# Sample states of a two-layer HGRN2 and SSD decoder step: the queries moved to four column tiles, the new states to two row tiles

## What is computed

```python
o_inter = jnp.einsum('bthk,bhkv->bthv', qb * jnp.exp(G), s)          # HGRN2, 4 heads, 128x128
s_new = jnp.exp(g_last)[..., None] * s + jnp.einsum('bshk,bshv->bhkv', k_dec, vb)
y_inter = jnp.einsum('btgn,bgrnp->btgrp', cb, hg) * jnp.exp(acum)[..., None]   # SSD, 8 heads, 128x64
h_new = jnp.exp(a_last)[..., None, None] * hg + jnp.einsum('bsgn,bsgrp->bgrnp', bb, xg * w[..., None])
```

## Time and profile before

| | |
|---|---|
| runs, us | 1828.41 median of 3 (1827.68 to 1837.21) |
| the profiled execution, us | 1836.97, its span 1835.2 |
| TensorE busy | 1779.1 us, 97% of the span |
| VectorE, ACT, GpSimd busy | 71%, 56%, 6% |
| mean granted TensorE clock | 0.963 |

### The profile page before, as it was taken

How to read it: one execution, slowest core, us unless ns; L and a number is a source line. 1 busy time by engine, 2 the same in 40 slices (tenths; PEclk the granted TensorE clock), 3 DMA queues, 4 the chain that set the end, 5 groups by cost and what they waited for, 6 DMA issues and landing times.

```text
span 1835.2 us, 23214 instructions
## 1 busy us (share of the span) xinstructions
PE 1779.1 (97%) x9594; PEld 1549.2 (84%) x9594; DVE 1296.9 (71%) x1099; ACT 1036.0 (56%) x934; POOL 112.1 (6%) x101
## 2 busy tenths in 40 slices
PE   8999999999999998998999999999999999899997
PEld 7988888999999978886888878888788888788886
DVE  6635555444347345547988888888988888788897
ACT  4443224333334342227777777777777777677776
POOL 2011120000000011210400000000000000000200
PEclk9998879999999978788999999999999999999999
DMA  9458144443453512137999999999999999899994
GB/s 291 160 180 241 35 111 147 141 158 107 137 172 116 161 40 54 41 90 257 380 395 395 394 363 387 365 375 393 375 362 363 370 397 378 297 383 365 383 385 186
DMA packets 272616, 474.20 MB, mean 258 GB/s; under 512 B 41578, under 2 KB 103266, under 8 KB 272504
## 3 DMA queue, kind: packets, MB, share of 16 engines
q1 hardware_dynamic: 266432, 452.50, 69.5%
q10 hardware_dynamic: 3368, 12.75, 2.1%
q0 software_dynamic: 2704, 7.39, 1.4%
HBM read 454.82 MB, written 29.84 MB: 264 GB/s over the span
## 4 chain that ended last, share of the span: by engine, by line
PE 93%; DVE 4%; ACT 1%; issue 1%; DMA 0%; DVEq 0%; ACTq 0%
PE ps L1676 17%; PE ps L1677 17%; PE ps L2297 11%; PE ps L1671 9%; PE ps L1672 9%; PE ps L2318 5%; PE ps L1770 4%; PE ps L2183 3%; PE ps L1880 3%; PE ps L1865 2%; PE ps L2201 1%; PE ps L2336 1%; PE ps L1918 1%; PE ps L2145 1%; PE ps L2035 1%
## 5 line engine op out<-in xcount | busy, mean ns | idle before, releaser
L1556 DVE TENSOR_TENSOR spL<-ring,spH 128x2048 fp32r<-128x2048 f32 x336 | 767.3, 2292 | 111.2 <-ACT spH L954 106.4
L954 ACT ACTIVATE spH<-ring 128x2048 fp32r<-128x2048 f32 x336 | 643.4, 1917 | 136.3 <-PE ps L2297 74.0
L1676 PE MATMUL ps<-spH,XH 128*128 128x512 f32 x896 | 356.5, 398 | 1.9 <-issue 1.9
L1677 PE MATMUL ps<-spH,XL 128*128 128x512 f32 x896 | 352.5, 393 | 2.3 <-issue 2.3
L1037 DVE TENSOR_TENSOR spL<-ring,spH 128x2048 fp32r<-128x2048 f32 (+1 forms) x74 | 158.8, 2146 | 182.3 <-ACT spH L660 182.1
L1671 PE MATMUL ps<-hnH,spH 128*128 128x320 f32 x928 | 277.3, 313 | 4.1 <-DVE hnL L1052 2.2
L1672 PE MATMUL ps<-hnL,spH 128*128 128x320 f32 x928 | 275.6, 311 | 0.0
L2297 PE MATMUL ps<-spL,XH 128*128 128x512 f32 x896 | 242.5, 393 | 0.2 <-DVE spL L1556 0.2
L660 ACT ACTIVATE spH<-ring 128x2048 fp32r<-128x2048 f32 (+1 forms) x74 | 133.4, 1803 | 187.9 <-PE ps L2183 73.6
L1677 PEld LDWEIGHTS ps<-spH,XL 128*128 128x128 f32 x896 | 169.0, 189 | 38.4 <-issue 2.7
L2297 PEld LDWEIGHTS ps<-spL,XH 128*128 128x128 f32 x896 | 168.6, 188 | 38.6 <-DVE spL L1556 0.9
(11 more groups left out here) (358 smaller groups left out, 1944.0 us busy)
## 6 DMA issues: line engine op xcount, KB each, us to landing
ring<-in_w_exp_in_dram SPq DMA_DIRECT2D x224, 1024.0 KB, 8.1
ring<-in_w_exp_out_dram SPq DMA_DIRECT2D x112, 1024.0 KB, 8.5
ring<-in_w_in_dram SPq DMA_DIRECT2D x28, 1024.0 KB, 5.3
ring<-in_w_ffn_in_dram SPq DMA_DIRECT2D x22, 1024.0 KB, 5.1
token_rows<-token_rows ACTq DMA_DIRECT2D x1, 11776.0 KB, 41.9
ring<-in_w_ffn_out_dram SPq DMA_DIRECT2D x16, 704.0 KB, 4.6
ring<-in_w_out_dram SPq DMA_DIRECT2D x8, 1024.0 KB, 5.1
out_dram<-ring SPq DMA_DIRECT2D x32, 256.0 KB, 2.6
```

Of the source, the lines that this page charges most:

```text
L954: A(esplit(j)[0], src, ACT.Copy).then_inc(S("hi_done"), 1)
L1556: V.tensor_tensor(lo, eslot(j)[0], hi.bitcast(F32), ALU.subtract).then_inc(S("split_done"), 1)
L1676: mm(out, x[0], w, start=start, stop=False)
L1677: return mm(out, x[1], w, start=False, stop=False)
```

## The change

Queries: `ask(k, half)` serves four sequences at once, in two calls per group k (0 HGRN2, 1 SSD). The stationary side is now a block of 32 query columns (four sequences), the moving side the slab's 128 columns; head h writes to partitions 32h to 32h+31 of bank 5, which is column tile h of the array. 16 matmuls a call; of each block of 32 rows only the 8 of the slab's own sequence are used. ACT copies bank 5 to `said` (`told`), TensorE turns it with four transposes (`turn_said`), VectorE adds it to oT (`add_told`) or multiplies it for SSD (`decay_told`). `ASK_AT` and `TOLD_AT` place these.

New states: one call per pair of sequences j and j+4. Rows 0 to 31 of keys and values hold sequences 0 to 3, rows 32 to 63 sequences 4 to 7, and the mask `turn` keeps j in the one and j+4 in the other; the two halves are two row tiles (32 rows x 128 columns) and write to banks 4 and 7. All calls use the same two banks, so `sample_state(j)` waits until both adds of j-1 are done, and `sample_ssd(j)` too. `sample_ssd(3)` stays behind `group_squares(1)`, and the adds that it waits for stand on VectorE behind the scaling of oT.

```diff
+    turn = ((i[:, None] // LSQ) % 4 == np.arange(4)[None, :]).astype(np.float32)
...
-SEQ_AT = {(0, 1): (0,), (0, 2): (1,), (0, 3): (2,), (1, 1): (3,), (1, 2): (4, 5), (1, 3): (6, 7)}
-SEQ_BANK = (4, 7, 7, 4, 7, 4, 7, 4)
-SSD_BANK = (7, 4, 7, 7, 4, 7, 4, 7)
+SEQ_AT = {(0, 3): 0, (1, 1): 1, (1, 2): 2, (1, 3): 3}
+SEQ_BANK = (4, 7)
+SLABS = [8 * k + 4 * g + j for k in range(2) for j in range(4) for g in range(2)]
+ASK_AT = {(0, 1): 0, (0, 3): 1}
+TOLD_AT = {(0, 2): 0, (1, 0): 1}
...
+                for j in range(4):
+                    if j == 0:
                         pool.wait_ge(S("tab_in"), 16)
                         pool.wait_ge(S("kd_done"), LT(l, 2) + 1)
...
+                    nc.gpsimd.tensor_scalar(kdm[:, j], kd2[:], tabv("turn")[0:NS, j:j + 1], None, ALU.mult
+                                            ).then_inc(S("mask_done"), 1)
                 def decay_ssd(b):
...
+                    pool.wait_ge(S("state_mm"), l * 8 + 4 + b % 4 + 1)
                     sv = slab(l, 8 + b).rearrange("p (h v) -> p h v", h=NH)
                     eb = ea[:, b * NH:(b + 1) * NH].unsqueeze(2).broadcast_to([P, NH, HD])
                     nc.gpsimd.tensor_tensor(sv, sv, eb, ALU.mult).then_inc(S("slab_dec"), 1)
...
+                for j in range(4):
+                    if j == 0:
                         pool.wait_ge(S("Bt_done"), LT(l, 2) + 1)
                         pool.wait_ge(S("ea_exp"), 2 * l + 1)
...
+                        pool.wait_ge(S("state_mm"), l * 8 + 4)
+                    nc.gpsimd.tensor_scalar(Bm[:, j], Btt[2][:], tabv("turn")[0:NS, j:j + 1], None, ALU.mult
+                                            ).then_inc(S("mask_done"), 1)
+                for j in range(4):
+                    decay_ssd(j)
+                    decay_ssd(4 + j)
...
+                def decay_state(j):
+                    act.wait_ge(S("state_mm"), l * 8 + j + 1)
+                    for b in (j, 4 + j):
+                        for h in range(H):
+                            c = slice(h * P, (h + 1) * P)
+                            ins = A(slab(l, b)[:, c], slab(l, b)[:, c], ACT.Copy, scale=egl[:, h, b:b + 1])
+                        ins.then_inc(S("slab_dec"), 1)
+                def told(k, half):
+                    act.wait_ge(S("ask_mm"), 4 * l + 2 * k + half + 1)
+                    if k == half == 0:
+                        act.wait_ge(S("conv_stored"), 32 * (l + 1))
+                    A(said[k][:], ps[:, 5, :], ACT.Copy).then_inc(S("said_done"), 1)
...
+                    if (t, h) in ASK_AT:
+                        told(0, ASK_AT[t, h])
+                    if (t, h) in SEQ_AT:
+                        decay_state(SEQ_AT[t, h])
...
-                act.wait_ge(S("hg_o"), l + 1)
+                act.wait_ge(S("told_done"), 4 * l + 2)
...
+                told(1, 0)
                 steps_decay(0)
                 turned_tokens(1)
+                told(1, 1)
...
+                def told_views(x, g, half):
+                    mine = x[:, :, 32 * g + 16 * half:32 * g + 16 * half + 16].rearrange("p h (j r) -> p h j r", j=2)
+                    o = 5 * 512 + 256 * g + 16 * half
+                    pair = ps[:].rearrange("p b n -> p (b n)")[:, o:o + 2 * (P + LSQ)].rearrange("p (j q) -> p j q", j=2)
+                    return mine, pair[:, :, 0:P].rearrange("p j (h m) -> p h j m", h=H)[:, :, :, 0:LSQ]
+                def add_told(half):
+                    dve.wait_ge(S("said_tr"), 4 * l + half + 1)
+                    dve.wait_ge(S("o_evac"), LT(l, 2) + 1)
+                    for g in range(2):
+                        mine, theirs = told_views(oT[:, :, NPR:TOK], g, half)
+                        ins = V.tensor_tensor(mine, mine, theirs, ALU.add)
+                    ins.then_inc(S("told_done"), 1)
+                def decay_told(half):
+                    dve.wait_ge(S("said_tr"), 4 * l + 2 + half + 1)
+                    dve.wait_ge(S("E_exp"), 2 * l + 1)
+                    for g in range(2):
+                        mine, theirs = told_views(t2[:], g, half)
+                        ins = V.tensor_tensor(mine, told_views(EE2[:], g, half)[0], theirs, ALU.mult)
+                    ins.then_inc(S("told_done"), 1)
+                def add_ssd(j):
+                    for g in range(2):
+                        b = 4 * g + j
+                        dve.wait_ge(S("slab_dec"), 16 * l + 8 + 2 * j + g + 1)
+                        V.tensor_tensor(slab(l, 8 + b), slab(l, 8 + b), ps[:, SEQ_BANK[g], :], ALU.add
+                                        ).then_inc(S("slab_done"), 1)
...
-                add_ssd(0)
                 within(2)
+                decay_told(0)
                 step_gates(1)
                 mixing(0)
-                add_ssd(1)
+                add_ssd(0)
                 dve.wait_ge(S("gsq_done"), 2 * l + 1)
                 V.tensor_tensor(oT[:], oT[:], ogT[:], ALU.mult).then_inc(S("og_done"), 1)
                 inputs(1)
-                add_ssd(2)
                 within(0)
...
                 mixing(1)
-                add_ssd(3)
-                add_ssd(4)
+                decay_told(1)
+                dve.wait_ge(S("told_done"), 4 * l + 4)
+                join(2, t2)
                 across(1, 2, 0)
+                add_ssd(1)
                 within(1)
-                join(1)
+                join(1, t1)
...
+                V.tensor_tensor(cvT[:, 0:4], cvT[:, 0:4], zT[:], ALU.mult).then_inc(S("z_done"), 1)
                 dve.wait_ge(S("grs_done"), 2 * l + 1)
                 dve.wait_ge(S("og_done"), l + 1)
                 for h in range(H):
                     ins = V.scalar_tensor_tensor(out=oT[:, h], in0=oT[:, h], scalar=vec[:, l, 56 + h:57 + h],
...
-                add_ssd(5)
-                add_ssd(6)
+                add_ssd(2)
                 dve.wait_ge(S("mixH_done"), 2 * l + 1)
                 V.tensor_tensor(hnL[:, 0:4], oT[:], hnH[:, 0:4].bitcast(F32), ALU.subtract
                                 ).then_inc(S("mixL_done"), 1)
-                add_ssd(7)
-                across(2, 1, 5)
-                join(2)
-                V.tensor_tensor(cvT[:, 0:4], cvT[:, 0:4], zT[:], ALU.mult).then_inc(S("z_done"), 1)
+                add_ssd(3)
...
+                def ask(k, half):
+                    if k == half == 0:
                         pe.wait_ge(S("qG_done"), H * (l + 1))
...
+                        if l:
+                            pe.wait_ge(S("told_done"), 4 * l)
+                    elif (k, half) == (1, 0):
+                        pe.wait_ge(S("conv_done"), 8 * (l + 1))
+                        pe.wait_ge(S("told_done"), 4 * l + 2)
+                    else:
+                        pe.wait_ge(S("told_done"), 4 * l + 2 * k + half)
+                    pe.wait_ge(slab_in[2 * k], 16 * 4 * (l + 1))
+                    pe.wait_ge(slab_in[2 * k + 1], 16 * 4 * (l + 1))
+                    for g in range(2):
+                        for j in range(2):
+                            b = 4 * g + 2 * half + j
+                            o = 4 * g * LSQ
+                            for h in range(H):
+                                q = qG[:, h, o:o + 32] if k == 0 else cvT[:, 6 + h // 2, NPR + o:NPR + o + 32]
+                                m = mm(ps[32 * h:32 * h + 32, 5, (2 * g + j) * P:(2 * g + j + 1) * P],
+                                       q, slab(l, 8 * k + b)[:, h * P:(h + 1) * P], start=True, stop=True)
+                    m.then_inc(S("ask_mm"), 1)
+                def turn_said(k, half):
+                    pe.wait_ge(S("said_done"), 4 * l + 2 * k + half + 1)
+                    for i in range(4):
+                        m = nc.tensor.transpose(ps[:, 5, i * P:(i + 1) * P], said[k][:, i * P:(i + 1) * P], ident)
+                    m.then_inc(S("said_tr"), 1)
+                def sample_state(j):
+                    if j == 0:
+                        pe.wait_ge(S("lfL_done"), LT(l, 1) + 1)
                         pe.wait_ge(S("sh_done"), 2 * l + 1)
...
+                    elif j == 1:
                         pe.wait_ge(S("v_done"), LT(l, 1) + 1)
...
                         pe.wait_ge(S("kd_done"), LT(l, 1) + 1)
                     else:
...
+                        pe.wait_ge(S("slab_done"), 16 * l + 2 * j)
+                    pe.wait_ge(S("mask_done"), 8 * l + j + 1)
                     for h in range(H):
...
+                        for g in range(2):
+                            rows_g = slice(32 * g, 32 * g + 32)
+                            m = mm(ps[:, SEQ_BANK[g], h * P:(h + 1) * P], kdm[rows_g, j, h * P:(h + 1) * P],
+                                   vtk2[rows_g, h * P:(h + 1) * P], start=True, stop=True)
+                    m.then_inc(S("state_mm"), 1)
...
+                def sample_ssd(j):
+                    pe.wait_ge(S("mask_done"), 8 * l + 4 + j + 1)
+                    if j == 0:
                         pe.wait_ge(S("xw_done"), LT(l, 2) + 1)
...
```

(31 more changed lines are left out.)

111 lines of the change are left out of this document (22 added, 89 removed).

## The result

The changed kernel takes 1782.84 us (median of 4 runs, 1776.59 to 1788.33) where the kernel before, on the same chip, takes 1830.88: a ratio of 0.9732, 95% interval 0.9688 to 0.9777, 48 us less. The forecast was 1810 with a range from 1795 to 1826: the direction was right, the gain more than twice as large as the 18 us of the sum. Two further sets of runs of the same kernel gave 0.9717 (0.9682 to 0.9752) and 0.9759 (0.9726 to 0.9792). The profiled execution took 1781.33 us.

A forecast was written before the change was run, and what follows sets the result against it. TensorE, busy 97% of 1835.2 us, bounds the kernel. Heads -7.5, SSD up to the sums -2.4, behind them +0.9: -9.0 us a layer, -18 for two, from 1828.4 to 1810, range 1795 to 1826.

The forecast's parts named there:

- with the same share of half-clock time: Heads and SSD: half-clock share stays, so its loss shrinks only with the work, -1.0 and -0.5 us a layer.
- Rival 1: Mixers' clock gets better as 128-column calls replace 8-column query groups: 12 to 14 us more, 1798; chance 0.17.
- Rival 2: Clock gets worse from idle TensorE and bare waits: 2 us each in 4 phases, 1818; chance 0.13.
- DMA ... I count nothing: HGRN2 slabs wanted together load without recorded TensorE waits, stores only change order; GpSimd's decays stay ahead: nothing counted.
- The prices of the calls: TensorE in both mixers, per call: queries 1.4 us, HGRN2 states 1.3 us, SSD states 1.2 us.
- Rivals 3 and 4: Mixer calls: row tiles don't overlap, 1823, chance 0.13; no tiles overlap, slower than before, 1840, chance 0.07.
- The Trainium skill's rule that the prediction weighed: Query calls: about 62 ns sequencing per matmul with hardware decode off, 2.0 us a call; set aside for 1.4.
- Transposes: TensorE, 4 calls a layer turning the query results: 0.44 us each, 1.8 us in all.
- Waits in the heads: TensorE's waits for VectorE in the heads part go from about 5.3 to 5.7 us a layer, +0.4.
- inside(0): SSD part: decay_told(0) ahead on VectorE waits for the transposes, giving inside(0) 0.5 us extra wait.
- Behind the sums: After group_squares(1): last state call starts after some 6 us idle, ends 0.7 to 0.9 us late; +0.9 a layer.
- The signs of being wrong: Query group over 2.5 us, SSD clock outside 0.70 to 0.85, or last Bm group over 2 us behind hnL.

The follow-up runs named there:

- the first four rows: The kernel before; it plus an unread table, 1819.97 us; third weight buffer alone moved, 1824.88 us; unread table with that buffer held back, 1829.25 us.
- the four changed ones: The changed kernel, 1782.84 us; two unaltered repeats, 1781.62 and 1787.99 us; and it with 8 more unread columns in its table, 1790.57 us.
- wide: Kernel before with its queries streaming 64 columns instead of 8, extra results overwritten or unread: 1816.77 us, ratio 0.9867.
- queries alone: Kernel before with the new four-column-tile queries, transposes, adds and early product with zT, but the old states per sequence: 1800.09 us, ratio 0.9783.
- kept alone: Kernel before with the unread table, third weight buffer (spH2, spL2) alone put back at offset 32 in 64 bytes: 1829.25 us, ratio 0.9984.
- padded: Changed kernel with 8 more unread columns in table turn, moving the tiles behind it 32 bytes more: 1790.57 us, ratio 0.9719.
- second run: The changed kernel once more, unaltered, as the measure for runs beside it: 1781.62 us, ratio 0.9717 to the kernel before.
- third run: The changed kernel a third time, unaltered, on another chip: 1787.99 us, ratio 0.9759 to the kernel before.

## Why the prediction was wrong

The 48 us, from the table of the mixers (means of the first four rows and of the four changed ones) and the ends:

| part | forecast | measured |
|---|---|---|
| work and waits in the mixers (rest 198.3 to 177.8) | -15 | -20.5 |
| half level in the mixers (lost 31.4 to 17.9) | -3 | -13.5 |
| experts (mean end of before, wide, queries alone, kept alone, padded 1036.5; of the three runs of the changed one 1027.0) | 0 | -9.5 |
| sum | -18 | -43.5 |

Some 4 us of the medians' difference are not assigned; they are less than the interval. Whole executions say the same of the rest and more of the clock: in the second and third run of the changed kernel the rest is 29 and 32 us less (the 20.5 and the 9.5 above), and what is lost is 27 and 9 us less, by what the kernel before loses on that chip. So the sum was short by half even where the clock gave little.

- **The step that failed first: "with the same share of half-clock time"** (-1.0 a layer in the heads, -0.5 in SSD). The loss fell by 13.5 us instead. Rival 1, which had 0.17 and 12 to 14 us (half of 21 and a third of 12 are 14.5), was right in cause and size; the time ended below its 1798 because the other parts were short too. I had the observation for it (the half level follows 8-column rows) and set it aside because no row showed what counts. Two neighbouring calls in the kernel before would have shown it: behind 193.49 TensorE is never idle and still falls to the half level. The wide queries show that columns, not fewer matmuls, make the difference. Rival 2 (waits make it worse) is there as well: in the changed kernel's profile half-level stretches of SSD stand at the wait of 2.69 us (218 to 225 us) and inside that of 5.60 (from 239 us). In the second run the state call behind the new 2.18 us wait takes longer as well, with a granted clock of 0.62,

```profile
188.40 1.75 PE L1973 MATMUL ps<-vtk,kdm 32*128 32x128 f32 x16 [2.18 <-DVE ring L1372]
```

  and that run loses 5.6 us more than the first. The same wait of 2.18 us stands in the first run with the clock at 1.00 behind it, so the wait alone doesn't decide; what does isn't shown.
- **"DMA ... I count nothing" and nothing for the tables.** The change's one line of constants moved the third weight buffer and all else behind the tables by 32 bytes, some 10 us in a part that no step of the prediction looked at. No row of before could have given it; that the change adds to a table was there to be seen in the diff.
- **The prices of the calls** were mis-sized in one direction: queries 1.01 for 1.4 (four calls, 1.6 us a layer), HGRN2 states 1.09 for 1.3 (0.8), SSD states 1.07 for 1.2 (0.4). 2.8 us a layer, 5.6 in all, as much as the difference between -15 and -20.5; the smaller misses below about cancel. Both prices were taken from rows with two column tiles. Four tiles and alternating row tiles overlap more: 0.032 us a record, under a third of a full array's 0.107, and a state call of 16 records costs what 8 cost before. Rivals 3 and 4 are out, and would come true in part if the order were the other one. The Trainium skill's rule that the prediction weighed (TensorE: Matmul & The Clock Gate, section "Wait — 56ns, not 53.3ns?") holds where hardware decode is off, and would have made the call 2.0 us. The trace has 1.01, so the rule doesn't bind here; whether decode was off is not on record.
- **Transposes** 0.43 to 0.56 us a call for 0.44: 0.3 us a layer short. **Waits in the heads** 2.18, 1.93, 1.11 and 0.59, 5.8 us in all for 5.7: right.
- **inside(0)** waits 2.69 us for M where I had 0.5 us more than before's small wait: too small by 1 to 2 us a layer, hidden in a part that gained by its clock.
- **Behind the sums** the last state call waits 5.60 us (about 6) and ends 0.5 us behind hnL (0.7 to 0.9), but the stretch from the sums to `projected(0)` is 8.95 us against 9.2: -0.3 where I had +0.9.
- **The signs of being wrong** did not warn. A query group takes 1.01 us and not over 2.5, the SSD clock is 0.84 and so inside 0.70 to 0.85, and the last `Bm` group ends 0.5 us behind hnL and not 2. The heads' clock, which went from 0.92 and 0.90 to 1.00, was not among them.

## What to carry over

Where TensorE's clock is low although it is busy, look at what it streams: here groups of matmuls with 8 moving columns cost the same as with 64, and the clock that they lost was worth more than the instructions (queries alone: 34 us less lost, the rest 10 us less). Small matmuls overlapped fully where neighbours went to different tiles, and less where 8 records of one tile stood in a row, so put the loop over tiles innermost. And before a gain is put down to an edit, count the instructions in a stretch that the edit doesn't touch: a new constant can move a buffer. Where the granted clock of every execution is on record, split each time into lost and rest before comparing: the rest of one program agrees within 3 us between chips here, the time of the kernel before only within 10 (1831 to 1841).

## What was not expected of the hardware

- A matmul's pace in the experts depends on the address of its operands: 1793 to 1797 in 400 us with the third weight buffer at an offset of 32 in 64 bytes, 1806 with it alone at 0, 1810 to 1814 with the other tiles moved too, all at full clock and busy 397.8 us. 32 bytes are worth 6 to 9 us of 1780 to 1830.
- 32 records on four column tiles of 32 take 1.01 us in turn and 2.39 us tile by tile.
- A column tile call at the half level (granted clock 0.50) takes 1.94 us, at the full one 1.08: short matmuls in tiles feel the clock almost wholly.
- The same program loses 14.3 or 19.9 us to the half level in its mixers in two executions, and 27 to 37 with the same narrow queries. Over whole executions of the kernel before it is 51 to 77 us. One profile of each kernel isn't enough to size it.
